# Attention slots of a decoder block: value products of the previous head ahead of the turning of this head's probabilities

## What is computed

```python
q = rmsnorm(q.reshape(B, T, N_HEADS, HEAD_DIM), q_gain[i])
k = rmsnorm(k.reshape(B, T, N_HEADS, HEAD_DIM), k_gain[i])
y_att = moba_attention(q, k, v, slopes)   # softmax(q k / 8 - slope * distance), causal, times v
h = h + jnp.concatenate([y_lru, y_att], axis=-1) @ w_out[i]
u = rmsnorm(h, ln_ffn[i])
g_up, v_up = jnp.split(u @ w_up[i], 2, axis=-1)
```

## Time and profile before

| quantity | us |
|---|---|
| median of 3 runs | 634.01 |
| lowest and highest of them | 633.53, 634.43 |
| the profiled execution, its own time | 634.09 |
| its span in the trace | 632.3 |

### The profile page before, as it was taken

How to read it: one execution, slowest core, us unless ns; L and a number is a source line. 1 busy time by engine, 2 the same in 40 slices (tenths; PEclk the granted TensorE clock), 3 DMA queues, 4 the chain that set the end, 5 groups by cost and what they waited for, 6 DMA issues and landing times.

```text
span 632.3 us, 7947 instructions
## 1 busy us (share of the span) xinstructions
PE 627.9 (99%) x2885; PEld 521.5 (82%) x2885; DVE 438.4 (69%) x650; ACT 337.3 (53%) x492; POOL 362.1 (57%) x267
## 2 busy tenths in 40 slices
PE   9999999999999999999999999999999999999997
PEld 7887788888888888888888888888888888888886
DVE  3692499978748797769734477697354677989574
ACT  5779953878836455546333345453343364457341
POOL 6684433743307537499664454996644559963370
PEclk9999999999999999999999999999999999999999
DMA  8742335471103644303546223045462222652022
GB/s 297 289 136 98 101 100 133 123 203 61 41 1 121 242 171 167 100 1 102 132 137 233 97 100 101 1 119 128 154 230 76 99 95 93 170 172 100 34 84 83
DMA packets 22934, 77.80 MB, mean 123 GB/s; under 512 B 2672, under 2 KB 3184, under 8 KB 22640
## 3 DMA queue, kind: packets, MB, share of 16 engines
q1 hardware_dynamic: 21456, 72.45, 34.3%
q0 software_dynamic: 1296, 4.72, 4.0%
q10 hardware_dynamic: 144, 0.13, 0.1%
HBM read 64.83 MB, written 4.19 MB: 109 GB/s over the span
## 4 chain that ended last, share of the span: by engine, by line
PE 99%; DVE 0%; issue 0%; POOL 0%; POOLq 0%
PE psum L1519 30%; PE psum L1521 30%; PE psum L1520 30%; PE psum L1715 2%; PE psum L1701 1%; PE psum L1661 1%; PE psum L1565 1%; PE psum L1568 1%; PE psum L1573 1%; PE psum L1598 1%; PE psum L1848 1%; PE psum L1631 1%; PE psum L1616 1%; PE psum L1682 0%; PE psum L1558 0%; PE psum L1658 0%
## 5 line engine op out<-in xcount | busy, mean ns | idle before, releaser
L505 POOL TENSOR_TENSOR wlo<-raw,whi 128x512 fp32r<-128x512 f32 x82 | 112.9, 1377 | 192.3 <-ACT whi L591 191.9
L1521 PE MATMUL psum<-uhi,wlo 128*128 128x512 f32 x488 | 189.8, 389 | 0.0
L1520 PE MATMUL psum<-ulo,whi 128*128 128x512 f32 x488 | 189.8, 389 | 0.0
L1519 PE MATMUL psum<-uhi,whi 128*128 128x512 f32 x488 | 189.8, 389 | 0.0
L506 POOL TENSOR_TENSOR wlo<-raw,whi 128x512 fp32r<-128x512 f32 x82 | 117.6, 1434 | 0.0
L591 ACT ACTIVATE whi<-raw 128x1024 fp32r<-128x1024 f32 x78 | 81.9, 1054 | 58.0 <-PE psum L1521 57.3
L1520 PEld LDWEIGHTS psum<-ulo,whi 128*128 128x128 f32 x488 | 91.6, 188 | 19.1
L1519 PEld LDWEIGHTS psum<-uhi,whi 128*128 128x128 f32 x488 | 91.6, 188 | 19.1
L1521 PEld LDWEIGHTS psum<-uhi,wlo 128*128 128x128 f32 x488 | 91.6, 188 | 18.9
L837 ACT ACTIVATE tmp<-psum,vec 128x512 f32<-128x512 f32 x24 | 16.6, 690 | 84.3 <-DVE psum L1293 84.3
L1364 DVE TENSOR_TENSOR ws<-raw,held 128x1024 f32<-128x1024 f32 x24 | 47.1, 1987 | 9.3 <-POOL elo L557 9.1
(11 more groups left out here) (253 smaller groups left out, 1183.9 us busy)
## 6 DMA issues: line engine op xcount, KB each, us to landing
raw<-in_weights SPq DMA_DIRECT2D x94, 512.0 KB, 3.3
held<-in_weights SPq DMA_DIRECT2D x12, 512.0 KB, 5.7
wlo<-ws POOLq DMA_DIRECT2D x6, 512.0 KB, 5.9
xtok<-in_x SPq DMA_DIRECT2D x4, 512.0 KB, 8.8
out<-first SPq DMA_DIRECT2D x1, 2048.0 KB, 8.7
back<-out SPq DMA_DIRECT2D x1, 2048.0 KB, 7.7
first<-in_x_t SPq DMA_DIRECT2D x7, 256.0 KB, 7.1
raw<-in_weights SPq DMA_DIRECT2D x7, 256.0 KB, 7.1
```

What stands on the lines that cost most here:

```text
L505: nc.gpsimd.tensor_tensor(wlo[s][:, 0:CW // 2], raw[s][:, 0:CW // 2], whi[s][:, 0:CW // 2].bitcast(F32), ALU.subtract)
L1519: mm(o, ahi, bhi, start=start, stop=False, skip_group_check=shared)
L1520: mm(o, ahi, blo, start=False, stop=False, skip_group_check=shared)
L1521: return mm(o, alo, bhi, start=False, stop=stop, skip_group_check=shared)
```

## The change

In each slot h of 1 to 7 the value products of head h-1 are issued ahead of the turns of head h. Slot 0 has no value products and stays as it is. No instruction is added or removed, no wait's number changes, and the streams of the other engines stay the same.

```diff
             for h in range(HEADS):
-                turn_probs(h)
                 if h:
                     values(h - 1)
+                turn_probs(h)
                 if h + 3 < KD:
                     out_lru(h + 3)
```

## The result

| | us |
|---|---|
| kernel before, median of 20 runs | 633.96 |
| changed kernel, median of 20 runs | 635.34 |
| ratio | 1.0020, 95% interval 1.0013 to 1.0026 |
| the same in a second set of runs (11 against 33) | 634.92 against 634.03, ratio 1.0016, interval 1.0007 to 1.0025 |
| profiled execution of the changed kernel, its span | 635.42, 633.6 |

One of the 20 runs of the changed kernel took 1062.55 us at a mean granted clock of 0.558; the ratio is formed without it, and no trace of it was kept.

A forecast was written before the change was run, and what follows sets the result against it. TensorE's instruction stream was taken to bound the kernel. Seams of -0.38 us and a new wait of 1.15 us sum to +0.77 us, a median of 634.8 us (+0.12%), with an 8-in-10 range of 633.8 to 635.9.

The forecast's parts named there:

- TensorE's stream is the time: TensorE, busy 627.9 of 632.3 us, sets the time; each microsecond it waits in the slots is one at the end.
- The seams: Changed neighbours in TensorE's stream: 0.05 us gained in each of slots 1 to 6, 0.08 in slot 7, 0.38 together.
- the upper bound of the wait: Slot 7's new wait at 1.3 us, if first distances after it are as long as at other seams.
- The chain that shifts once and keeps its lag: ScalarE and VectorE work starting from the turns comes 1.23 us later once and doesn't fall further back.
- The room of the tightest long slot: Values at the head of slot 4 wait for slot 3's sum, with 0.80 us left after the shift.
- The wait of slot 7: values(6), at the head of slot 7, wait 1.15 us (0.9 to 1.3) for the sum made in slot 6.
- A second wait behind it: None expected: slot 7's filler has 0.26 us of room, values(7) 0.35; 0.3 us kept at the upper end.
- That the wait isn't there: Rival: slot 6 causes no wait and only the seams count, about 633.6 us; 10%.
- Waits in the long slots: Rival: growing lag makes values wait there, some 0.3 us in each of four slots, 636.0 us; 16%.
- the clock rival: Slot 7's wait drops the granted clock to 1.2 GHz around its filler and values: +4.2 us, 638.2 us; 2%.

The follow-up runs named there:

- the trial: New order in slots 1 to 4 only, VectorE making the first remainder of head 3 twice or three times: 634.48 and 635.07 us beside 633.90.
- the two kernels with the sum first: Changed kernel, slot 6 moving and summing head 5 first: 634.67 us; also three filler matmuls moved from slot 5 to 6: 634.40; both beside 634.10.
- slot 6 alone: New order in slot 6 only, other slots as in the kernel before: 635.05 us, ratio 1.0014.
- slots 1 to 5: New order in slots 1 to 5 only, slots 6 and 7 as in the kernel before: 634.21 us beside 634.03, ratio 1.0005.
- the run with the sum first: Changed kernel, but in slot 6 the move and sum of head 5 come ahead of head 6's copies and remainders: 634.67 us beside 634.10.

## Why the prediction was right, and what was mis-sized

**That TensorE's stream is the time, without slack behind it.** Right. The stretch is 1.08 us longer, and the span of two executions of the changed kernel differs from that only by the start.

**The seams, -0.38 us forecast, -0.21 measured.** This is the larger of the two misses. Slots 1 to 5 take 170.67 - 139.23 = 31.44 us against 170.60 - 138.99 = 31.61 before, -0.17 instead of -0.25; slot 6 up to the wait 3.72 against 3.75; slot 7 5.16 (175.67 to 180.83) against 5.17. (139.23 and 138.99 are where slot 1 begins in either timeline.) Values behind scores take 1.22 us and not 1.31, so the seam that was to go away did. But the turns behind values take 1.03 us instead of 1.01, and the filler's first distance is 0.32 instead of 0.31. The earlier trace rows already had turns of 1.03 us ahead of a filler (133.97 to 135.00), and the working passed over them. In slot 7 the values follow a wait, and their first distance is 0.30 us (175.67 to 175.97), as long as behind turns: the wait gave that seam back. The forecast had this only in the upper bound of the wait.

**The chain that shifts once and keeps its lag.** Right. ScalarE idles 0.62 and 0.33 us before the copies of slots 4 and 5, as it did before (0.65 and 0.35). Counted from the start of the slot, copies come 1.2 us later in each, and no slot from 1 to 5 has a wait.

**The room of the tightest long slot, 0.80 us forecast.** The time between the end of the sum and the values is 157.97 - 157.23 = 0.74 us here, and by the trial 0.57 us count. Between these two stands the release, which I left out of this step though I had it in the next. It cost nothing, since nothing needed that room.

**The wait of slot 7, 1.15 us forecast, 1.28 measured.** The start of the values, counted from the start of slot 6, was put at 4.85 us and is 5.00 (175.67 - 170.67). By links, measured against forecast: turns 1.21 for 1.23; copies 0.66 for 0.64; remainders 0.64 for 0.63; their length 1.62 for 1.62; sum +0.03 for -0.08; its length 0.69 for 0.69; release 0.15 for 0.12. The failed link is the sum's start: I took the overlap of 0.08 us from slot 5. Slot 5 adds an even head (head 4), slot 6 an odd one (head 5), and these differ in both traces. VectorE of the changed kernel in slots 4 and 5, where heads 3 and 4 are added:

```profile
161.03 1.61 DVE L1248 TENSOR_TENSOR prTlo<-psum,prThi 128x512 fp32r<-128x512 f32 x3
162.67 0.69 DVE L1239 TENSOR_TENSOR tmp<-psum,tmp 64x512 f32<-64x512 f32 x1
...
167.53 1.62 DVE L1248 TENSOR_TENSOR prTlo<-psum,prThi 128x512 fp32r<-128x512 f32 x3
169.07 0.67 DVE L1239 TENSOR_TENSOR tmp<-psum,tmp 64x512 f32<-64x512 f32 x1
```

The sum of head 3 starts 0.03 us after the shown end of the remainders, that of head 4 0.08 us before it, 0.11 us of difference. Odd heads write partitions 64 to 127, even heads 0 to 63. The Trainium skill, VectorE: DVE Perf Modes, section "Two Vector instructions with no wait between them", says that a Vector instruction that starts at another quadrant (a group of 32 partitions) than the one before is held until all earlier ones have finished. The rows agree with it, and so do the two kernels with the sum first: the remainders, which start at partition 0, start 0.04 and 0.03 us after the shown end of the sum of head 5 (172.77 to 172.81, 172.81 to 172.84). No run here changed the partitions alone, so that the quadrant is the reason is argued, not shown.

**A second wait behind it.** Right, there is none: the filler of slot 7 and the values of head 7 start in the usual spacing. Their inputs are ready 0.39 us (177.61 against 178.00) and 0.37 us (180.46 against 180.83) ahead of them, where 0.26 and 0.35 were forecast. The release of the filler's low part had 0.15 us of room before and shows how near this was: it waits as soon as the sum comes late in another way (slot 6 alone, slots 1 to 5).

**The rivals.** That the wait isn't there fell by the trace. Waits in the long slots fell too, and the trial with two and three remainders shows their deciding point at 0.57 us. The granted clock stayed in the top tenth in every slice of the trace of the changed kernel, and also in the kernels with the turns 3 and 6 matmuls later, which have four waits of up to 0.87 us and eight of up to 0.93 us as shown in and behind these slots (their mean clocks are 0.999 and 1.000). So the clock rival fell in every trace that was kept. The rule of the Trainium skill that was cited for it (TensorE: Matmul & The Clock Gate, section "A second HAM failure mode: psum-queue depth-cycling") speaks of frequent pauses; eight of them didn't bring the clock down here, and whether more would isn't shown. The price of this rival was also put too low: by its own rows the filler of slot 7 and the values on both sides take 2.84 + 2 x 1.21 = 5.26 us, which at half the clock is an estimate of 5.3 us more and not of 3.4.

**Why the medians differ by 1.38 us in the first set and 0.89 in the second.** The stretch says 1.08 in both traces. The start of the kernel scatters by 0.7 us between executions (7.92 to 8.63 above), and the intervals of both ratios hold 1.08 us. The second trace also speaks against a cost ahead of the slots, since its turns of head 0 stand 0.47 us earlier than before the change. In all fourteen traces here they stand between 133.50 and 134.20, and the kernel before, at 133.97, is among them.

## What to carry to other kernels

An operation issued earlier on the bounding engine is worth no more than its seams when its consumers queue behind the operation that it overtook; write the consumers' queues beside each other before moving anything. A lag that fits in the long rounds of a pipeline is paid in its shortest one, so check the last rounds first, where the filler runs out. And when an experiment moves an operation past another, list every wait whose room changes, at both ends of the move.

## What the runs showed of the hardware

A matmul after a wait for VectorE started 0.15 us after the shown end of the VectorE instruction (175.52 to 175.67, 158.65 to 158.80), where the one example before had 0.12. The first distance between two matmuls of 512 columns is 0.30 to 0.32 us behind transposes and 0.30 to 0.33 us behind a wait (the 0.33 in the run with the sum first, 174.48 to 174.81), against 0.23 in a stream. Ten transposes of 128 columns take 1.03 to 1.04 us behind a matmul of 128 columns and mostly 1.01 behind one of 256 or 512 columns; in slot 0 they take 1.03 to 1.04 behind one of 512, for a reason that no run here shows.
